# A two-layer attention and S5 step on one core: the S5 state copies and sums planned one unit nearer to the scan

## What is computed

```python
h = rmsnorm(x) * (1 + scale) + shift           # scale, shift, gate = silu(cond) @ w_ada
# layer 0: q, k, v, z = h @ w_in;  o = attention(q, k, v);  x += gate * ((o * silu(z)) @ w_out)
# layer 1: u, z = h @ w_in
#   s5, both directions, 128 groups of 16 channels, 64 complex states a group:
#   s[t] = a * s[t-1] + B u[t];   y = gelu(Re(C s) + d * u)
#   y = y * sigmoid(y @ w_glu + b_glu);  x += gate * ((y * silu(z)) @ w_out)
# out: rmsnorm(x), new keys and values, final s5 states
```

## Time and profile before

| | |
|---|---|
| median of 3 runs | 1176.69 us (1173.47 to 1179.65) |
| profiled execution, its own time | 1177.27 us |
| its span | 1175.4 us |
| TensorE busy | 1099.6 us (94%) |
| DVE busy | 755.5 us (64%) |
| ACT busy | 570.0 us (48%) |
| DMA | 325.04 MB, 277 GB/s mean |

### The profile page before, as it was taken

One profiled execution on the slowest core, in us unless ns is written; L12 is line 12 of the kernel. 1 busy time (PEld: TensorE's weight loads), 2 busy tenths in 40 slices (PEclk: granted clock), 3 DMA queues, 4 the chain that ended last, 5 costly groups with the idle time before them and its releaser, 6 DMA issues.

```text
span 1175.4 us, 17368 instructions
## 1 busy us (share of the span) xinstructions
PE 1099.6 (94%) x6786; PEld 827.6 (70%) x6786; DVE 755.5 (64%) x1207; ACT 570.0 (48%) x802; POOL 216.6 (18%) x378
## 2 busy tenths in 40 slices
PE   3799999999999999999999979999898998899995
PEld 0356777677777777778767656888686876788884
DVE  4146766766575765677588765379966894475663
ACT  5233534444433444345443455566768486355443
POOL 2001220344032501222234340100020211100000
PEclk9798999999999999999999989999898998999998
DMA  9999687888889987866798876877482866855551
GB/s 355 420 414 413 246 308 267 331 327 329 309 314 385 347 325 271 329 242 202 282 347 338 324 281 218 284 225 255 132 271 95 283 218 238 323 185 169 199 191 72
DMA packets 64113, 325.04 MB, mean 277 GB/s; under 512 B 9408, under 2 KB 16192, under 8 KB 32032
## 3 DMA queue, kind: packets, MB, share of 16 engines
q1 hardware_dynamic: 44176, 266.51, 61.2%
q0 software_dynamic: 12944, 46.94, 11.5%
q10 hardware_dynamic: 6912, 10.49, 2.5%
HBM read 295.55 MB, written 28.34 MB: 276 GB/s over the span
## 4 chain that ended last, share of the span: by engine, by line
PE 76%; DVE 8%; DMA 7%; ACT 6%; issue 3%; SPq 0%; ACTq 0%; DVEq 0%
PE ps L803 20%; PE ps L805 19%; PE ps L804 18%; PE ps L677 6%; DMA araw<-in_wada 4%; DMA raw<-in_w 3%; DVE wlo L1465 2%; ACT whi L1069 2%; PE ps L912 2%; PE ps L786 1%; PE ps L752 1%; PE ps L935 1%; PE ps L735 1%; DVE sb L1583 1%; PE ps L683 1%
## 5 line engine op out<-in xcount | busy, mean ns | idle before, releaser
L1465 DVE TENSOR_TENSOR wlo<-raw,whi 128x1024 fp32r<-128x1024 f32 x288 | 352.0, 1226 | 301.9 <-ACT whi L1069 297.7
L1069 ACT ACTIVATE whi<-raw 128x1024 fp32r<-128x1024 f32 x288 | 302.8, 1058 | 447.5 <-PE ps L805 432.1
L803 PE MATMUL ps<-whi,xhi 128*128 128x512 f32 x1152 | 471.5, 409 | 5.9 <-DVE xlo L1484 4.2
L805 PE MATMUL ps<-whi,xlo 128*128 128x512 f32 x1152 | 454.7, 395 | 0.0
L804 PE MATMUL ps<-wlo,xhi 128*128 128x512 f32 x1152 | 454.3, 394 | 0.0
L803 PEld LDWEIGHTS ps<-whi,xhi 128*128 128x128 f32 x1152 | 219.5, 191 | 90.4 <-issue 28.8
L805 PEld LDWEIGHTS ps<-whi,xlo 128*128 128x128 f32 x1152 | 219.1, 190 | 48.8
L804 PEld LDWEIGHTS ps<-wlo,xhi 128*128 128x128 f32 x1152 | 219.9, 191 | 41.7
L677 PE MATMUL ps<-araw,cT 128*32 128x512 f32 x640 | 81.5, 621 | 5.7 <-DMA araw<-in_wada 5.7
L677 PEld LDWEIGHTS ps<-araw,cT 128*32 128x32 f32 x640 | 16.5, 110 | 47.3 <-issue 28.8
L619 POOL DMA_DIRECT2D ctab<-ctab_scratch x16 | 8.6, 540 | 190.8 <-PE ps L935 190.8
(11 more groups left out here) (208 smaller groups left out, 1071.9 us busy)
## 6 DMA issues: line engine op xcount, KB each, us to landing
raw<-in_w SPq DMA_DIRECT2D x144, 1024.0 KB, 5.7
araw<-in_wada SPq DMA_DIRECT2D x80, 1024.0 KB, 8.5
raw<-in_wada SPq DMA_DIRECT2D x16, 1024.0 KB, 8.6
ctab_scratch<-ce POOLq DMA_DIRECT2D x16, 512.0 KB, 7.7
btab_scratch<-bs ACTq DMA_DIRECT2D x32, 256.0 KB, 4.3
btab<-btab_scratch SPq DMA_DIRECT2D x16, 512.0 KB, 4.0
ctab<-ctab_scratch POOLq DMA_DIRECT2D x16, 512.0 KB, 5.0
par<-in_par POOLq DMA_DIRECT2D x32, 128.0 KB, 6.3
```

Source lines behind the costliest of these rows:

```text
L803: mm(acc, xhi[:, kt, st], whi[:, s, k], start=kt == 0, stop=False)
L805: last = mm(acc, xlo[:, kt, st], whi[:, s, k], start=False, stop=kt == KT - 1)
L1069: af(whi[:, k % 4].rearrange("p k c -> p (k c)"), src, ACT.Copy).then_inc(s_hi, 1)
L1465: tt(wlo[:, slot, k % 2].rearrange("p k c -> p (k c)"), src, whi[:, k % 4].rearrange("p k c -> p (k c)").bitcast(F32), ALU.subtract).then_ ...
```

## The change

Four parts. (1) `scan_plan` returns the state copies at the unit of the last scan step instead of the one after (`ends[w] = k`), and the sums of group w+2 one unit after that step instead of two. (2) A double step is planned at 1.54 instead of 1.85, so that a unit's room of 2.8 takes two of them more often; the steps themselves and their instructions are the same. (3) For the last group, u is ordered at unit 195 instead of 196 and transposed at 196 instead of 198, and its outputs are made one quarter a unit instead of two. (4) The last tile of the GLU's input goes to PSUM bank 6 instead of 7, with a wait for the copy that empties bank 6.

The tables become `S_AT` (176, 184, 195, 204), `HY_AT` (194, 203, 214, 222), `Y_AT` (198, 207, 217, 225); the last scan step is at unit 222. Double steps are planned at units 188 to 194 (12 of them), 199 to 203 (9) and 208 to 214 (13), where before they were at 188 to 195 (12), 201 to 205 (8) and 211 to 218 (12). The positions of the GLU's tiles (`X_AT`) and of the products with z (`YZ_AT`) stay. On SP, three of the last group's four table loads (L407) move ahead by one piece of weights.

```diff
-ORDER_AT = tuple(UB * (B_IN1 + 1 + w) + 4 for w in range(NW))
-U_AT = tuple(x + 2 for x in ORDER_AT)
-TICK, TICKS2, PER_UNIT = 1.11, 1.85, 2.8
+ORDER_AT = tuple(UB * (B_IN1 + 1 + w) + (4 if w < NW - 1 else 3) for w in range(NW))
+U_AT = tuple(x + (2 if w < NW - 1 else 1) for w, x in enumerate(ORDER_AT))
+TICK, TICKS2, PER_UNIT = 1.11, 1.54, 2.8
...
-                    ends[w] = k + 1
+                    ends[w] = k
                     if w + 2 < NW:
-                        sums[w + 2] = k + 2
+                        sums[w + 2] = k + 1
...
-X_BANK = ((5, 6, 5, 6, 5, 6, 5, 6), (4, 4, 7, 7, 5, 6, 7, 5), (6, 7, 5, 6, 7, 5, 6, 7), (5, 7, 4, 7, 7, 7, 7, 7),
+X_BANK = ((5, 6, 5, 6, 5, 6, 5, 6), (4, 4, 7, 7, 5, 6, 7, 5), (6, 7, 5, 6, 7, 5, 6, 7), (5, 7, 4, 7, 7, 7, 7, 6),
...
 def quarters_at(starts, k):
 
-    return [(w, q) for w, x in enumerate(starts) for q in range(4) if x + (q // 2 if w == NW - 1 else q) == k]
+    return [(w, k - x) for w, x in enumerate(starts) if 0 <= k - x < 4]
...
                     if g == 0:
                         pe.wait_ge(s_uTsb, 2 * NW)
                         pe.wait_ge(s_Ssb, 4 * 4 * NW)
+                    if g == TG - 1:
+                        pe.wait_ge(s_fso, 1)
```

## The result

| | before | after |
|---|---|---|
| median of the runs | 1176.69 us (1173.47 to 1180.10, 5 runs) | 1186.22 us (1182.91 to 1188.53, 5 runs) |
| ratio | | 1.0072, 95% interval 1.0051 to 1.0092 |
| profiled execution | 1177.27 us, span 1175.4 | 1186.22 us, span 1184.4 |

The changed kernel is slower by 8.5 us by the ratio (interval 6.0 to 10.8; the two medians are 9.5 apart); the forecast was 1183.7, with a range of 1170 to 1191. The ends of the scans, the waits and their places came out close to the forecast. The loss is 2.1 us larger than the forecast's sum of 6.4.

The account below looks back on a forecast made before the run. It took the S5 stretches as bound by ACT and DVE, with TensorE ending the chain. Lag 9.7 minus tile gain 3.3 gave +6.4 us on the profiled 1177.27, so 1183.7 us, range 1170 to 1191.

Parts of the forecast that it names:

- The ends of the scans: S5 part, DVE: group scans end at 830.4, 880.1 and 937.0 us, counted from double steps of 1.64 and splits of 1.15.
- Group 2's sums: Second quarter's sums on TensorE start at 840.6 us behind unit 196, before at 840.78 behind unit 198; 5.3 us lost.
- lag: An event's time after the change minus before, plus TensorE work moved behind it; 9.7 us when all outputs are done.
- Group 3's last sums: Done at 903.9 us behind unit 207, where before these sums started at 908.26 behind unit 210; lag 3.9 us.
- Group 2's outputs: Gelu done at 952.0 us with a silu now in ACT's chain; new TensorE wait of 6.5 behind unit 218, lag 10.1.
- Group 3's outputs: One quarter a unit: wait of 3.4 us behind unit 226, all outputs done at 1001.8 behind unit 228, lag 9.7.
- The last tile: Tile moved to bank 6 no longer waits for the previous tile's `xlo`: gain 3.3 us, bounds 0 and 3.34.
- The slow restarts: TensorE runs slowly after a wait, costing 0 to 3.3 us each; four counted before and four after, at old prices.
- Restarts at full speed: Rival: TensorE comes back from its S5 waits at full speed, giving about 1178 us; chance 0.20.
- The chain catching up: Rival: ACT delivers as early as TensorE asks, group 2's second-quarter sums start before 836, total 1165.3 us; chance 0.15.
- A late piece of weights: Rival: ACT waits for weights within group 2's or 3's state copies, +5 us, about 1189 us; chance 0.10.
- The drain behind a table load: Rival: another 1.28 to 1.38 us behind each of four loads in groups 2 and 3, +5.3, 1189 us; chance 0.03.

Follow-up runs that it names:

- the silu experiments: Block 26's silu moved out of the chain in the changed kernel (1178.88 us, ratio 1.0008), and into it in the kernel before (1180.64 us, ratio 1.0030).

## Why the prediction was right, and where its sizes were off

*The ends of the scans* stood at 830.4 (forecast 830.4), 880.5 (880.1) and 937.3 (937.0): the timeline of DVE has

```profile
830.80 0.29 DVE L1591 COPY fs<-sb 128x32 f32<-128x32 f32 x2
...
880.83 0.28 DVE L1591 COPY fs<-sb 128x32 f32<-128x32 f32 x2
...
937.66 0.28 DVE L1591 COPY fs<-sb 128x32 f32<-128x32 f32 x2
```

with 0.36 to take off. Counting DVE's steps and splits was enough for these. TensorE's waits for the splits of units 194 and 195 were 1.39 each, forecast 1.7.

*Group 2's sums* came at 840.7 behind unit 196, forecast 840.6, a lag of 5.4 against 5.3. The transposes of u wait 3.14 (forecast 3.5), and the sums then 3.13.

*Group 3's last sums* came at 904.3 behind unit 207, forecast 903.9; the lag is 4.3 against 3.9. Here is the first size that was off: the sums and unit behind the long wait took 849.73 - 841.05 = 8.7 us where the row of before had 8.05, since the clock had been low since the transposes at 836.

*Group 2's outputs.* Wait for the split 1.55 (forecast 1.8), gelu done at 952.7 (952.0), wait behind unit 218 of 6.38 (6.5). The lag is 10.9, forecast 10.1. (The terms of that step add to 15.2 from 937.0, so 952.2, not the 952.0 written.) The mechanism, a silu now inside the chain, is what the silu experiments show from both sides. The step has the silu, the gelu's load and the slow restart behind the wait, each as a term of its own. What it didn't say is that all three hang on the silu's place: taking it out of the chain gave back 7.5.

*Group 3's outputs.* Wait 3.49 behind unit 226 (3.4); gelu done at 989.9 (988.7), all outputs done at 1003.5 (1001.8), both behind the units forecast. The lag is 11.5 instead of 9.7. By the trace the end is 1.7 us late: 0.8 was there at 952.8, another 0.1 by the end of unit 222 (973.0 against 972.1), 0.3 came up in ACT's chain to the gelu, and 0.5 from there to the last outputs, most of it in the slow restart (7.1 against 6.9) and the outputs behind it (6.4 against 6.2).

*The last tile* gave 3.3 - 0.5 = 2.8, since 0.51 of wait for `xlo` came up at the tile of unit 233; alone it gave its 3.3.

*The slow restarts.* "I count four again, at the prices of those rows" was right in number (836, 890, 953, 990) and not in size: 17.1 us of lost clock against 12.0. By the stretches shown, group 3's sums have one instead of two, -1.7 (3.4 against 5.1); that of group 2's sums is longer by 3.2, of which 1.6 fell on the 3.13 us in which TensorE was idle; and that at 953 is 3.2 where nothing was.

So 6.4 forecast, 11.5 - 2.8 = 8.7 in the trace, 8.5 in the ratio. Of the 2.3 between forecast and trace 1.8 lie in the lag and 0.5 in the tile. These misses are on the same side, so they did not cancel out to make the hit.

*The rivals.* Restarts at full speed: no, the clock fell behind all four waits. The chain catching up: no, the sums began at 840.7, not before 836. A late piece of weights: ACT did wait 3.99 for one, at 934.39, but waited 2.53 more for the end of the scan behind it, so it cost the chain nothing. The drain behind a table load (three more of them than before, where the prediction counts four, since one load stood in group 2's chain before): the silu starts 945.60 - 944.31 = 1.29 after the start of its load and the gelu 952.65 - 951.36 = 1.29, with nothing in between. The Trainium skill (ScalarE: Activation LUTs, "What ACT_TABLE_LOAD costs") gives 2.66 for a switch; the trace does not agree, at any of the loads shown here.

## What to carry to other kernels

When a chain on ACT and DVE keeps its length, planning it nearer doesn't shorten it: it takes away the TensorE work beside it. One unit farther can lose too, when something with a fixed place, here a silu and a tile that reads a transfer, then meets the chain. Look for what can leave the chain before moving the chain: one silu cost its own 2.4 us, a second table load, and the low clock behind a longer wait. And try each line of a change alone: the bank was a gain that the loss of the plan hid, and one quarter a unit is a gain in the kernel before once its tile has room. But read the trace of such a run for waits that only it has: 1.54 without the earlier transposes of u made ACT stand still for 8.14 us, and its total alone would have blamed the dense steps.

## What I had not expected of the hardware

The low clock comes to more than half of TensorE's waits (12.0 us lost against 20.2 in the kernel before, some of it while TensorE was idle). It falls to 0.50, that is from 2.4 to 1.2 GHz, and stays there after TensorE has come back. The longest such time in these traces is 13.6 us (6.8 lost, from 835 to 850 in the changed kernel). Behind waits of 3.14, 3.49, 4.46, 6.38 and 7.26 the first matmuls ran at the low level, behind 4.08 and 2.46 only later ones, behind 2.62 none. Length alone doesn't decide it: behind the 3.34 of the last tile there was nothing slow, and behind 2.00 there was the earlier trace rows. Nor is it the same each time: with the silu of block 26 moved out, the same wait of 3.14 was followed by transposes near full speed (1.09 us instead of 1.97; the clock was low only behind them). What decides, the runs don't show.
